# Local attention in pairs of heads in a one-core block kernel, and a third pair of PSUM banks in two projection stages

## The reference

```
s_band = einsum('bnqkgd,bnskd->bnkgqs', qb, kband) * scale + bias_band       # window of 128 keys back
s_band = where(mask_band, s_band, NEG)
s_meta = einsum('bnqkgd,bmkd->bnkgqm', qb, k_meta) * scale + bias_m          # the 16 meta keys
s_meta = where(dist_m >= 0, s_meta, NEG)
p = softmax(concatenate([s_meta, s_band, sink], axis=-1), axis=-1)           # sink: one logit a head
out = einsum('bnkgqm,bmkd->bnqkgd', p_meta, v_meta) + einsum('bnkgqs,bnskd->bnqkgd', p_band, vband)
```

## Time and profile before

| | |
|---|---|
| median of 3 runs | 1700.89 us |
| the profiled execution | 1700.79 us |
| its span | 1699.0 us |
| TensorE busy | 1635.6 us (96%) |
| VectorE, ScalarE, GpSimd busy | 1118.9, 928.6, 211.5 us |
| chain that ended last | TensorE 87%, VectorE 7%, ScalarE 4% |

### The profile page before, as it was taken

The page is one execution under the profiler, slowest core; times in us unless marked ns, Lnnn a source line. Parts: engine busy times, 40 slices in busy tenths (PEclk is TensorE's granted clock), DMA queues, the critical chain, the costliest instruction groups (busy, mean ns, idle before and its releaser), DMA issues.

```text
span 1699.0 us, 31760 instructions
## 1 busy us (share of the span) xinstructions
PE 1635.6 (96%) x12846; PEld 1579.8 (93%) x12846; DVE 1118.9 (66%) x2454; ACT 928.6 (55%) x2014; POOL 211.5 (12%) x218
## 2 busy tenths in 40 slices
PE   7999999999999999999899999899999888999998
PEld 7999989999999999999899998888898778989997
DVE  6555588786647876564487755854368867678862
ACT  5444364564436654375565544656575666566652
POOL 5000000000000000001100001044433662100000
PEclk9999999999999999999999999899999999999999
DMA  8554545555555555643355556533354324545551
GB/s 266 174 174 162 186 149 174 163 169 173 163 179 173 179 171 164 188 139 120 114 174 178 189 167 198 148 110 100 100 174 124 97 79 138 171 155 183 171 183 45
DMA packets 260210, 266.04 MB, mean 157 GB/s; under 512 B 4739, under 2 KB 259025, under 8 KB 260064
## 3 DMA queue, kind: packets, MB, share of 16 engines
q1 hardware_dynamic: 258528, 260.72, 48.4%
q0 software_dynamic: 1536, 3.29, 0.8%
HBM read 262.90 MB, written 1.09 MB: 155 GB/s over the span
## 4 chain that ended last, share of the span: by engine, by line
PE 87%; DVE 7%; ACT 4%; issue 2%; DMA 0%; POOL 0%; SPq 0%; DVEq 0%; ACTq 0%; POOLq 0%
PE ps L918 54%; PE ps L920 26%; DVE wl L2037 1%; ACT wh L1389 1%; DVE CY L2124 1%; PE ps L685 1%; DVE CY L2005 0%; PE ps L686 0%; PE ps L674 0%; DMA X<-in_x 0%; ACT swP L1128 0%; PE ps L751 0%; DVE SY L2010 0%; ACT EX L1337 0%; PE ps L719 0%
## 5 line engine op out<-in xcount | busy, mean ns | idle before, releaser
L2037 DVE TENSOR_TENSOR wl<-raw,wh 128x512 fp32r<-128x512 f32 x931 | 613.3, 708 | 309.3 <-ACT wh L1389 302.5
L1389 ACT ACTIVATE wh<-raw 128x512 fp32r<-128x512 f32 (+1 forms) x989 | 552.0, 618 | 210.0 <-PE ps L918 209.5
L918 PE MATMUL ps<-XH,wh 128*128 128x258 f32 (+3 forms) x2528 | 644.6, 290 | 10.6 <-ACT XH L1017 4.7
L920 PE MATMUL ps<-XH,wl 128*128 128x258 f32 (+3 forms) x2528 | 635.2, 287 | 0.0
L918 PEld LDWEIGHTS ps<-XH,wh 128*128 128x128 f32 x2528 | 481.6, 190 | 19.0 <-issue 11.8
L920 PEld LDWEIGHTS ps<-XH,wl 128*128 128x128 f32 x2528 | 480.9, 190 | 0.3
L918 PE MATMUL ps<-XL,wh 128*128 128x258 f32 (+3 forms) x2528 | 350.1, 288 | 0.0
L918 PEld LDWEIGHTS ps<-XL,wh 128*128 128x128 f32 x2528 | 326.0, 190 | 3.3 <-issue 2.4
L920 PE MATMUL ps<-HH,wl 128*128 128x272 f32 (+1 forms) x704 | 172.9, 283 | 0.0
L918 PE MATMUL ps<-HH,wh 128*128 128x272 f32 (+1 forms) x704 | 172.9, 284 | 0.0
L920 PEld LDWEIGHTS ps<-HH,wl 128*128 128x128 f32 x704 | 132.4, 188 | 0.0
(11 more groups left out here) (442 smaller groups left out, 2133.2 us busy)
## 6 DMA issues: line engine op xcount, KB each, us to landing
raw<-in_ffn_wg SPq DMA_DIRECT2D x44, 1024.0 KB, 5.3
raw<-in_ffn_wu SPq DMA_DIRECT2D x44, 1024.0 KB, 5.4
raw<-in_w_in SPq DMA_DIRECT2D x33, 1024.0 KB, 5.3
raw<-in_ffn_wd SPq DMA_DIRECT2D x32, 1024.0 KB, 5.1
raw<-in_w_ffn_in SPq DMA_DIRECT2D x22, 1024.0 KB, 5.1
raw<-in_ffn_wd SPq DMA_DIRECT2D x16, 768.0 KB, 4.7
raw<-in_conv_w_in SPq DMA_DIRECT2D x12, 1024.0 KB, 5.2
raw<-in_kv_w SPq DMA_DIRECT2D x8, 1024.0 KB, 5.4
```

The costliest lines, as they stand in the source:

```text
L918: mm = e.matmul(o, hi[:, k, c], xk, start=u.first and part == 0 and k == 0, stop=u.last and end)
L920: e.matmul(o, lo[:, k, c], xk, start=False, stop=False)
L1389: e.activation(wh[u.n % NH][:, c], raw[u.n % NR][:, c], ACT.Copy).then_inc(s_hi, 1)
L2037: e.tensor_tensor(wl[u.n % NR][:, c], raw[u.n % NR][:, c], wh[u.n % NH][:, c].bitcast(F32), ALU.subtract).then_inc(s_lo, 1)
```

## The change

Three edits.

1. The local attention runs over rounds r = 0 to 8, each with two heads (2r and 2r + 1) and six steps on every engine. `KZ` is replaced by `KK`, each key head in both halves of the rows without zeros. The scores of two heads are matmuls of 64 rows each, the first head in rows 0 to 63 and bank 4, the second in rows 64 to 127 and bank 5, one after the other in each of three shapes. The outputs of two heads go to the two halves of PS[7]'s partitions in turn, and the first of the three products reads 16 rows instead of 128 with zeros. The softmax operations of ScalarE are done per head, those of VectorE (maximum, sum, reciprocal) and GpSimd on both heads in one instruction; the scores' bias is added per head. Transposes stay as many; those into PS[7] of both heads go together. The rate is 4.9 and 54 steps are queued.
2. The convolution stage has three pairs of banks.
3. The stage kv2, dt, q2 has three pairs of banks.

In the diff, of the functions that are rewritten (`pe_swa`, `act_swa`, `dve_swa`) only the new lines stand. Left out are the edits that only take the local attention's cases out of helpers shared with the first block's attention.

```diff
         QR = [sb(st, f"QR{i}", [128, T]) for i in range(8)]
-        KZ = [[sb(st, f"KZ{p}{g}", [128, T]) for g in range(2)] for p in range(2)]
+        KK = [sb(st, f"KK{g}", [128, T]) for g in range(2)]
         VV, VN = sb(st, "VV", [128, T]), sb(st, "VN", [128, 3, 128])
-        sw = Softmax(st, "sw")
+        SS2, P2 = sb(st, "SS2", [128, 2, 432]), sb(st, "P2", [128, 2, 432])
+        PT0, PT1, PT2 = (sb(st, f"swPT{i}", [128, 2, n]) for i, n in enumerate((T, 256, 128)))
+        MX, NM, SM, RC, ES = (sb(st, f"sw{x}", [128, 2, 3]) for x in ("MX", "NM", "SM", "RC", "ES"))
+        NSK = sb(st, "NSK", [128, 16])
     with ExitStack() as st:
         YB = sb(st, "YB", [128, 16, NV])
...
     plan_norm(0)
+    P.ring = (0, 2, 4)
     for j in range(4):
         P.group(("c", j), A["conv_w_in"][0], KD, 1024 + 256 * j, 2, two(s_cr, 6 * j))
...
     P.run("ln5", 1)
+    P.ring = (0, 2, 4)
     P.group("kv2", W_IN, KD, K0, 2, two(s_cr, 24))
     P.group("dt", W_IN, KD, DT0, 1, [(s_cr, 27)])
...
     swa_free = P.bank[4], P.bank[5]
-    P.queue(sum(pipeline_steps(h, 16) for h in range(19)))
-    P.rate = 9
+    P.queue(6 * 9)
+    P.rate = 4.9
     for j in range(8):
...
+    def pe_swa(e, r):
+        if r < 8:
+            if r == 0:
                 e.wait_ge(s_kz, 4)
                 e.wait_ge(s_vm, 18)
                 e.wait_ge(*swa_free[0])
                 e.wait_ge(*swa_free[1])
             else:
+                e.wait_ge(s_s2, 8 + 2 * r)
+            e.wait_ge(s_cr, 27 + r + 1)
+            for c0, q0, q1, k1 in ((0, 144, 272, T), (272, 16, 144, 144), (416, 0, 16, 16)):
+                for par in range(2):
+                    hh = slice(64 * par, 64 * par + 64)
+                    mm = e.matmul(PS[4 + par][0:q1 - q0, c0:c0 + k1], QR[r][hh, q0:q1], KK[r // 4][hh, 0:k1],
+                                  start=True, stop=True)
+                    if c0 == 416:
+                        mm.then_inc(s_sc2, 1)
+        yield
+        for par in range(2):
+            if r:
+                if par == 0:
+                    e.wait_ge(s_pn, 16 + 3 * (r - 1) + 3)
+                    if r == 1:
+                        e.wait_ge(s_dtt, 5)
+                        e.wait_ge(s_csl, 1)
+                if r > 1 or par:
+                    e.wait_ge(s_p6, 16 + 2 * (2 * (r - 1) + par))
+                e.transpose(PS[6][0:16, 0:16], P2[0:16, par, 416:432], ident[0:16, 0:16])
+                e.transpose(PS[6][0:16, 16:144], P2[:, par, 272:288], ident[:])
+                e.transpose(PS[6][0:16, 144:272], P2[:, par, 0:16], ident[:])
+                e.transpose(PS[6][:, 272:400], P2[:, par, 144:272], ident[:]).then_inc(s_t6, 1)
+            yield
+        if r:
+            if r == 1:
+                e.wait_ge(s_d2, 1)
             else:
+                e.wait_ge(s_al, r - 1)
+            for par in range(2):
+                e.transpose(PS[7][:, 256 * par:256 * par + 128], P2[:, par, 288:416], ident[:])
+                tr = e.transpose(PS[7][:, 256 * par + 128:256 * par + 256], P2[:, par, 16:144], ident[:])
+            tr.then_inc(s_t7, 1)
+        yield
+        yield
+        if r:
+            e.wait_ge(s_p6, 16 + 4 * r)
+            e.wait_ge(s_p7, 8 + r)
+            gs = slice(64 * ((r - 1) // 4), 64 * ((r - 1) // 4) + 64)
+            for n, (n0, rows_, Pt) in enumerate(((0, 16, PT0), (16, 128, PT1), (144, 128, PT2))):
+                for par in range(2):
+                    mm = e.matmul(PS[7][64 * par:64 * par + 64, n0:T], VN[0:rows_, n, gs], Pt[0:rows_, par, :],
+                                  start=n == 0, stop=n == 2)
+            mm.then_inc(s_av, 1)
+        yield
...
+    def act_swa(e, r):
+        yield
+        for par in range(2):
+            if r:
+                e.wait_ge(s_t6, 8 + 2 * (r - 1) + par + 1)
+                if r > 1 and par == 0:
+                    e.wait_ge(s_av, 8 + r - 1)
+                e.activation(PT0[0:16, par, :], PS[6][0:16, 0:272], ACT.Copy).then_inc(s_p6, 1)
+                e.activation(PT2[:, par, :], PS[6][:, 272:400], ACT.Copy).then_inc(s_p6, 1)
+            yield
+        if r:
+            e.wait_ge(s_t7, 8 + r)
+            e.activation(PT1[:], src3(PS[7][:, :], 2), ACT.Copy).then_inc(s_p7, 1)
+        if r < 8:
+            e.wait_ge(s_nm, 8 + r + 1)
+            for par in range(2):
+                for q in (2, 1, 0):
+                    (c0, c1), n = COLS[q], 16 if q == 0 else 128
+                    e.activation(P2[0:n, par, c0:c1], SS2[0:n, par, c0:c1], ACT.Exp, bias=NM[0:n, par, q:q + 1],
+                                 accum_out=SM[0:n, par, q:q + 1])
+            e.wait_ge(s_es, r + 1)
+            e.activation(ES[:], ES[:], ACT.Exp).then_inc(s_ex, 1)
+        yield
+        yield
+        if r:
+            if r == 1:
                 e.wait_ge(s_csl, 1)
+            e.wait_ge(s_av, 8 + r)
+            e.activation(AH[:, r - 1, :], PS[7][:, TS:T], ACT.Copy).then_inc(s_ah, 1)
+        yield
...
         for g in range(2):
             for par in range(2):
-                e.activation(KZ[par][g][64 * par:64 * par + 64, :], QR[7][64 * g:64 * g + 64, :],
+                e.activation(KK[g][64 * par:64 * par + 64, :], QR[7][64 * g:64 * g + 64, :],
                              ACT.Copy).then_inc(s_kz, 1)
...
-        for b in (KZ[0][0], KZ[0][1], KZ[1][0], KZ[1][1], VN):
-            e.memset(b[:], 0.0)
-        for b in sw.MX + sw.SM:
-            e.memset(b[:], 0.0)
-        e.memset(sw.PT0[:], 0.0).then_inc(s_kz0, 1)
+        e.memset(MX[:], 0.0)
+        e.memset(SM[:], 0.0).then_inc(s_kz0, 1)
...
+    def dve_swa(e, r):
+        if r < 8:
+            if r == 0:
                 e.wait_ge(s_b, 64 + 80)
+                e.wait_ge(s_kz0, 1)
+                e.tensor_scalar(NSK[:], SNK[:], -1.0, None, ALU.mult).then_inc(s_sm, 1)
+            else:
+                e.wait_ge(s_ex, 16 + r)
+            for par in range(2):
+                h, S, o = 2 * r + par, PS[4 + par], SS2[:, par, :]
+                e.wait_ge(s_sc2, 8 + h + 1)
+                e.tensor_tensor(o[:, 0:272], S[:, 0:272], B2[:, h, ::-1], ALU.add)
+                e.tensor_tensor(o[:, 272:288], S[:, 272:288], B1[:, h, ::-1], ALU.add)
+                e.tensor_tensor(o[:, 288:416], S[:, 288:416], B2[:, h, 127::-1], ALU.add)
+                e.tensor_tensor(o[0:16, 416:432], S[0:16, 416:432], B0[:, h, ::-1], ALU.add).then_inc(s_s2, 1)
+        yield
+        yield
+        if r < 8:
+            e.wait_ge(s_s2, 8 + 2 * r + 2)
+            for q in (2, 1, 0):
+                (c0, c1), n = COLS[q], 16 if q == 0 else 128
+                e.tensor_reduce(MX[0:n, :, q], SS2[0:n, :, c0:c1], AX.X, ALU.max).then_inc(s_mx, 1)
+            e.wait_ge(s_mx, 16 + 3 * r + 3)
+            sink = NSK[:, 2 * r:2 * r + 2].unsqueeze(2).to_broadcast([128, 2, 3])
+            e.wait_ge(s_sm, r + 1)
+            e.scalar_tensor_tensor(out=NM[:], in0=MX[:], scalar=-1.0, in1=sink, op0=ALU.mult, op1=ALU.min).then_inc(s_nm, 1)
+            e.wait_ge(s_nm, 8 + r + 1)
+            e.tensor_tensor(ES[:], NM[:], sink, ALU.subtract).then_inc(s_es, 1)
+        yield
+        yield
+        if r < 8:
+            e.wait_ge(s_ex, 16 + r + 1)
+            e.tensor_tensor(SM[:], SM[:], ES[:], ALU.add).then_inc(s_sm, 1)
+            e.wait_ge(s_sm, r + 2)
+            if r:
+                e.wait_ge(s_pn, 16 + 3 * r)
+            e.reciprocal(RC[:], SM[:]).then_inc(s_rc, 1)
+        yield
+        if r:
+            e.wait_ge(s_ah, r)
+            e.tensor_tensor(AL[:, r - 1, :], PS[7][:, TS:T], AH[:, r - 1, :].bitcast(F32), ALU.subtract).then_inc(s_al, 1)
+        yield
...
-        for h in range(19):
-            yield from idle((h < 16) + (0 <= h - 3 < 16))
-            if 0 <= h - 1 < 16:
-                pool_normalise(e, sw, h - 1, 8, (2, 1, 0))
-                yield
-            yield from idle(2 * (0 <= h - 2 < 16) + (h < 16))
+        for r in range(9):
+            yield from idle(4)
+            if r < 8:
+                e.wait_ge(s_rc, 8 + r + 1)
+                for q in (2, 1, 0):
+                    (c0, c1), n = COLS[q], 16 if q == 0 else 128
+                    e.tensor_tensor(P2[0:n, :, c0:c1], P2[0:n, :, c0:c1],
+                                    RC[0:n, :, q:q + 1].to_broadcast([n, 2, c1 - c0]), ALU.mult).then_inc(s_pn, 1)
+            yield
+            yield
```

More of the change, by code:

```diff
@@ L340, in build @@
     s_kq, s_vmz, s_vt, s_vm = sem("kq"), sem("vmz"), sem("vt"), sem("vm")
-    s_sc2, s_sc1, s_s2, s_s1, s_s0 = (sem(n) for n in ("sc2", "sc1", "s2", "s1", "s0"))
+    s_sc2, s_sc1, s_s2, s_s1 = (sem(n) for n in ("sc2", "sc1", "s2", "s1"))
     s_mx, s_nm, s_ex, s_es, s_sm, s_rc, s_pn = (sem(n) for n in ("mx", "nm", "ex", "es", "sm", "rc", "pn"))
@@ L810, in pe_steps @@
         yield from idle(2)
-        for h in range(19):
-            yield from pe_swa(e, h)
+        for r in range(9):
+            yield from pe_swa(e, r)
         yield from idle(16 + 4)
@@ L1274, in act_steps @@
```

(37 more changed lines are left out.)

107 lines of the change are left out of this document (7 added, 100 removed).

## The result

| | before | after |
|---|---|---|
| median | 1700.71 us (4 runs) | 1677.78 us (4 runs) |
| lowest and highest | 1699.23, 1701.44 | 1676.49, 1678.94 |
| profiled execution | 1700.79 | 1678.86 |
| its span | 1699.0 | 1677.0 |

The ratio is 0.9866, its 95% interval 0.9849 to 0.9883. The change saves 22.9 us where 16.8 was forecast. By the interval of the ratio the saving is 19.9 to 25.7 us, so the 16.8 lie outside it. The sign is right, the time lies in the range, close to its lower end, and the total of rival (b), everything beside everything at 1679, is nearer than the forecast's.

The account below looks back on a forecast made before the run. TensorE, busy for 96% of the span, was taken to bound the kernel. Savings of 12.5 (attention in pairs) + 2.0 (convolution banks) + 2.3 (q2 banks) = 16.8 us from 1700.89 gave 1684, range 1677 to 1692.

Parts of the forecast that it names:

- rival (b): Whole kernel: everything runs beside everything, stalls stay at 2; 16.5 + 2.0 + 3.5 = 22 us saved, 1679; chance 0.17.
- Scores (1.5 a pair): Local attention: two heads' score visit falls from 2.08 to 1.5 us, bounds 1.28 to 2.3.
- The remark on the drain: Attention's visits: changing the tiling mode drains the engine, already inside 1.28 us; another 0.2 us a visit would lose 3 us.
- rows 7: Trace of before, state-space stage: one visit with two heads in the column halves, 432 columns, 1.28 us.
- Outputs (1.65): Local attention: two heads' output visit falls from 2.88 to 1.65 us a pair, saving 1.23.
- the transposes: Local attention: their number is unchanged and they take 1.54 us a pair.
- Stalls of the chain (4 us): Attention rounds: 0.3 us in each of seven inner rounds, 1 each for first and last pair; 4 against 2.1 before.
- GpSimd's 3.0 us: Softmax chain: GpSimd's three multiplications for a pair, taken as 3.0 us, between 1.88 and 3.76.
- part 1: Local attention, scores and outputs two heads at a time: net 12.5 us saved, between 5 and 16.5.
- Part 2 (2.0): Convolution stage, three bank pairs: the 2.04 us wait before b0 goes, 2.0 us saved, bounds 1.5 to 2.1.
- Part 3 (2.3): Before q2, three bank pairs: 4.36 us wait becomes waits at VV and L789; 2.3 us saved, between 1.0 and 4.3.
- The claim that the part is worth the same with and without a fall of the clock: Stage before z0: whether or not the clock falls in the stall at VV, three bank pairs save 2.3 us.

Follow-up runs that it names:

- The two experiments that lengthen TensorE's visits and nothing else: The kernel after with the scores' six matmuls in the order of heads, 1684.15 us; the same exchange in the outputs, 1687.07 us.
- The two kernels of the first experiments: The kernel after without both three-pair bank edits, 1684.07 us; the kernel before with three bank pairs in the convolution stage alone, 1697.76 us.
- the last experiment: The kernel after with three unused GpSimd multiplications of 128x544 elements ahead of each pair's normalisation: 1714.71 us, ratio 1.0089.
- the kernel with later side steps: The kernel after with the side work's credit at the start of q2 at -2.0 instead of 0: 1677.88 us, ratio 0.9865.

## Why the prediction was right, and where it missed

**The bound** was read rightly: TensorE's own queue. The two experiments that lengthen TensorE's visits and nothing else, by 8.2 and 11.1 us, move the end by 6.4 and 9.3.

**Scores (1.5 a pair).** 1.25. The prediction had set down that it is wrong if the score visit is at either end of its bounds, and the visit is at the lower end, 1.28, or a little past it. So by its own sign this term failed: its overlap was priced too low, and it is the largest error in TensorE's work. The lower bound, 1.28 from the visit of the state-space stage, was the better value: halves of the rows overlap as well as halves of the columns. The two orders of the same matmuls, 1.25 and 2.28 us, agree with another sentence of the Trainium skill (TensorEngine Tiling (Array Packing), Key Properties), that different tiles can load weights and multiply in parallel. The 0.25 that I laid on it for not having seen them costs 2.0 us in the sum. The remark on the drain at a change of the tiling mode (the Trainium skill, TensorEngine Tiling (Array Packing), Key Properties) held as it was put: the 1.25 us show nothing beyond what the 1.28 us of rows 7 contain.

**Outputs (1.65).** 1.57, and the transposes, by what is left of the stage (106.1 - 69.6 - 1.9 - 8 x 2.82 = 12.0), 1.50 a pair against 1.54: 0.9 us together.

**Stalls of the chain (4 us).** 1.9, which is the other large error: in the first and the last pair only, 1.11 and 0.78 us where 1 each was forecast; the inner rounds, for which 0.3 each stood, show none in the matmuls, and 0.9 us in two rounds in the weight loads ahead of them (2.8 us in four rounds, less the 1.9). The step of the chain that was mis-sized is GpSimd's 3.0 us, which is 1.9 to 2.4: I scaled the old operation, and the new one is another. That the margin is thin, as the chain's sum said, held. The end of GpSimd's normalisation stands this far ahead of TensorE's first transpose of it, for the pairs 0 to 7: 0.06 (after a wait), 0.06, 0.34, 2.02, 1.01, 0.06, 0.24, 0.05 (after a wait) us. In four inner rounds of six it is under 0.4 us. This is why 1.1 to 1.6 us more on GpSimd cost 7 us at once. With GpSimd at 3.0 us the kernel would stand near that experiment, whose two GpSimd stages together take 3.0 to 3.5 us a pair.

So part 1 is 17.5 and not 12.5: 2.0 scores, 0.6 outputs, 0.3 transposes, 2.1 stalls. Its upper bound was added up wrongly besides: with scores at 1.28 and stalls as before it is 12.5 + 1.8 + 1.9 = 16.2, not 16.5.

**Part 2 (2.0)** is 2.2 to 2.3 us in the traces where the clock holds behind the wait, and 3.8 against the one in which it falls.

**Part 3 (2.3).** Both waits are there, near the sizes forecast: 2.32 us for VV (2.3), 1.50 for ZD (1.9). The claim that the part is worth the same with and without a fall of the clock can be tested, because it went both ways. From the norm's sum (L778 before) to z0 it is 35.7 us before (1072.26 to 1107.93). In the kernel with head-by-head scores the clock fell behind the wait for VV and no wait for ZD shows: 32.9 (1070.6 to 1103.48). In that with one GpSimd operation more it held, and 1.49 us of wait for ZD show: 32.8 (1070.8 to 1103.62). In the profiled execution of after it held at VV and fell behind ZD, a third way that I had not thought of: 34.4. Its windows of TensorE, which stand against the earlier trace rows:

```profile
1075.00:1080.00 5.00, 4.29 (x35) 1.00 0.14 44
1080.00:1085.00 5.00, 4.46 (x36) 1.00 0.68 210
1085.00:1090.00 5.00, 4.04 (x24) 0.75 0.04 4
1090.00:1095.00 5.00, 5.00 (x37) 0.91 0.64 209
```

5 x 0.25 + 5 x 0.09 = 1.7 us of clock are lost here, about the difference between 34.4 and 32.8. So the claim held for a fall behind the first wait and not for one behind the second. The two kernels of the first experiments that keep two pairs of banks in q2 have 34.9 both, so the part is worth 2.1 us where the clock behaves alike. Single executions differ more: 2.8 from this one of before to 32.8, only 1.3 from it to the profiled one of after.

**The sum.** By the starts of the same matmuls in both traces, in the order of the program: 0.6 us ahead of the convolution stage, 2.2 in it, -1.3 up to the norm's sum (after has a stretch at 0.81 and 0.85 from 825 to 835, 1.7 us of clock, that before does not have), 1.3 up to z0, 17.5 in the attention, and 1.8 behind it (before has five microseconds at 0.70 from 1285, 1.4 us, that after does not have). That is 22.0 before rounding.

**The range** reached to 1677 because (b) was in it. The chance of 0.17 for (b) was too low: two of its three conditions, scores at 1.28 and stalls as before, were the nearest row's own value and came true (1.25 and 1.9), while the forecast had moved both towards caution. The third, 3.5 us for part 3, did not (2.1). That (b)'s total fits so well is partly luck: part 1 gave 1.0 us more than its 16.5, part 3 less, and what lies outside the three stages, in which the forecast had nothing, happens to give about 1 us in these two executions.

## What to carry to other kernels

Two small matmuls in different halves of TensorE's rows, or of its output's partitions, ran beside each other here only where they stood next to each other in the queue; halving the scores' rows without alternating them gained nothing here and cost 0.2 us a pair. When a whole trace has one visit of nearly the same shapes, take its time as the value, not as a bound to stay clear of. And when a change shortens a round of the bounding engine, measure the gap between the last producer of the round and its use: here it was 0.06 us in half the rounds, and a producer longer by 1.1 to 1.6 us gave a third of the gain back.

## What the runs showed of the hardware

**A stall of TensorE can cost more than its length, and not always.** A wait of 2.3 us for VV left the clock at 1.00 in after and in the kernel with one GpSimd operation more, and was followed by 0.67 and 0.66 in those with scores and outputs head by head, in the same five microseconds from 1075, though the four have the same instructions up to there. In the last experiment waits of 1.7 to 4.5 us, one a round, took 13.2 us of clock with them beside their own 25.5. Executions of one kernel differ in it too. The profiled one of the kernel with later side steps took 1673.09 us at a mean granted clock of 0.994 where its three others took 1677.45 to 1678.37 at 0.988 to 0.991. By the windows of 5 us below 0.97 of the clock that lie in its span it lost 9.1 us, the profiled one of after 15.5. So the spans of one pair of profiles can't settle an edit of 2 us such as parts 2 and 3; the length of its own stage in several traces, and its waits, can.

**Some instructions of VectorE last longer beside GpSimd's.** One piece of splitting on VectorE during GpSimd's normalisation (1160.96 to 1163.33), one small instruction during a piece of splitting on GpSimd, from the timeline of all engines of after:

```profile
1161.54 1.07 DVE L2044 TENSOR_TENSOR wl<-raw,wh 128x512 fp32r<-128x512 f32 x1 [0.66 <-ACT wh L1399]
...
1166.12 1.28 POOL L2429 TENSOR_TENSOR wl<-raw,wh 128x512 fp32r<-128x512 f32 x1 [1.56 <-ACT wh L1399]
1166.23 1.20 DVE L1845 SCALAR_TENSOR_TENSOR swNM<-swMX,NSK 128x6 f32<-128x6 f32 x1
```

Such a piece takes 0.67 us with GpSimd idle (at 1155.10), and L1845 took between 0.17 and 1.20 us; here it ends when GpSimd's instruction ends, at 1167.4. The longest piece, 2.96 us (at 1150.81), lies beside two pieces of GpSimd (1150.71 to 1153.21). In the stage the 24 pieces of VectorE take 0.93 us in the mean, against 0.72 before. L1831, which reads PSUM and one tile, takes 0.44 us beside GpSimd (at 1162.88) and 0.43 without it (at 1153.69). The Trainium skill (SBUF — State Buffer, SBUF: two separate sides) says that a VectorE operation with two inputs in SBUF and a GpSimd one that reads SBUF share a pair of ports, which one of them holds for its whole instruction. The trace agrees, as far as these rows go. I had not priced it, and it lies in the chain of each pair, in front of the exponentials. No run here took GpSimd's work away to test it.

**GpSimd's time is not a matter of elements alone.** By the rows by shape above, a column costs (964 - 642) / 128 = 2.5 ns in the product with a scalar and (1273 - 780) / 256 = 1.9 ns in the product of two tensors. Both are means of few instructions, some of which stood beside VectorE's.
